# The per-layer embedding stage: ScalarE's high parts at the top of a step, the weights' high part ahead of the square

## What is computed

```python
def rmsnorm(x, g):
    xf = x.astype(jnp.float32)
    xf = xf * lax.rsqrt(jnp.mean(xf * xf, axis=-1, keepdims=True) + EPS)
    return (xf * g.astype(jnp.float32)).astype(x.dtype)

def layer(...):
    ...
    x = x + jax.nn.sigmoid(rmsnorm(x, lw['ple_norm']) @ lw['ple_w_gate']) * (p_in @ lw['ple_w_proj'])
```

## Time and profile before

| | |
|---|---|
| median of 3 runs | 3121.93 us (3119.97 to 3122.65) |
| the profiled execution, its own time | 3125.64 us |
| its span, first to last instruction | 3123.9 us |
| mean granted TensorE clock | 0.976 of 2.4 GHz |
| PE busy | 2988.7 us (96%) |
| DVE busy | 1580.6 us (51%) |
| ACT busy | 1137.1 us (36%) |
| embedding stage of layer 0, from its step loop to its last matmul | 1442 to 1566 us of the span |
| embedding stage of layer 1, the same | 2981 to 3105 us of the span |

### The profile page before, as it was taken

The page is one execution under the profiler, slowest core; times in us unless marked ns, Lnnn a source line. Parts: engine busy times, 40 slices in busy tenths (PEclk is TensorE's granted clock), DMA queues, the critical chain, the costliest instruction groups (busy, mean ns, idle before and its releaser), DMA issues. The chain is left out here.

```text
span 3123.9 us, 46695 instructions
## 1 busy us (share of the span) xinstructions
PE 2988.7 (96%) x19219; PEld 2813.3 (90%) x19219; DVE 1580.6 (51%) x2696; ACT 1137.1 (36%) x2148; POOL 143.3 (5%) x260
## 2 busy tenths in 40 slices
PE   6999989999999999998989999999999999999997
PEld 5998755899999999998989887559999999999997
DVE  6233644564554554456561346445645554454655
ACT  6223423443333223335452333334533233333343
POOL 0000300000000000000000003000000000000000
PEclk9999889999999999998999989999999999999998
DMA  3101243421111111112221021533211111111021
GB/s 128 41 28 45 94 152 105 150 73 55 41 55 41 46 50 54 41 46 82 89 71 41 14 94 56 182 92 137 75 53 41 55 41 55 41 41 54 33 95 70
DMA packets 70742, 215.40 MB, mean 69 GB/s; under 512 B 6522, under 2 KB 43386, under 8 KB 54146
## 3 DMA queue, kind: packets, MB, share of 16 engines
q1 hardware_dynamic: 70530, 212.42, 19.7%
HBM read 193.52 MB, written 18.87 MB: 68 GB/s over the span
## 5 line engine op out<-in xcount | busy, mean ns | idle before, releaser
L223 PE MATMUL psum<-h_chunk,out_weight_parts 128*128 128x352 f32 x2112 | 681.5, 323 | 0.0
L224 PE MATMUL psum<-h_chunk,out_weight_parts 128*128 128x352 f32 x2112 | 677.1, 321 | 0.0
L225 PE MATMUL psum<-h_chunk,out_weight_parts 128*128 128x352 f32 x2112 | 676.4, 320 | 0.0
L2233 DVE SCALAR_TENSOR_TENSOR conv_sum<-u_padded,vectors,conv_sum 128x1024 f32<-128x1024 f32 x176 | 226.3, 1286 | 540.2 <-ACT conv_sum L2085 537.1
L224 PEld LDWEIGHTS psum<-h_chunk,out_weight_parts 128*128 128x128 f32 x2112 | 396.8, 188 | 0.0
L223 PEld LDWEIGHTS psum<-h_chunk,out_weight_parts 128*128 128x128 f32 x2112 | 396.2, 188 | 0.0
L225 PEld LDWEIGHTS psum<-h_chunk,out_weight_parts 128*128 128x128 f32 x2112 | 395.8, 187 | 0.0
L223 PE MATMUL psum<-g_parts,out_weight_parts 128*128 128x352 f32 x960 | 309.3, 322 | 0.0
L224 PE MATMUL psum<-g_parts,out_weight_parts 128*128 128x352 f32 x960 | 309.0, 322 | 0.0
L225 PE MATMUL psum<-g_parts,out_weight_parts 128*128 128x352 f32 x960 | 308.8, 322 | 0.0
L2259 DVE TENSOR_TENSOR x<-x,psum 128x352 f32<-128x352 f32 x528 | 254.9, 519 | 94.3 <-PE psum L225 94.0
(11 more groups left out here) (356 smaller groups left out, 5511.8 us busy)
## 6 DMA issues: line engine op xcount, KB each, us to landing
out_weight_stage<-w_up_dram SPq DMA_DIRECT2D x44, 1024.0 KB, 4.8
out_weight_stage<-w_down_dram SPq DMA_DIRECT2D x22, 1024.0 KB, 4.7
mix_weight_stage<-w_in_dram SPq DMA_DIRECT2D x18, 1024.0 KB, 4.9
pages<-cache_dram SPq DMA_DIRECT2D x64, 288.0 KB, 4.6
out_weight_stage<-w_out_dram SPq DMA_DIRECT2D x16, 1024.0 KB, 6.4
out_weight_stage<-w_gate_dram SPq DMA_DIRECT2D x16, 1024.0 KB, 4.8
pages<-cache_dram SPq DMA_DIRECT2D x64, 160.0 KB, 2.7
x<-x_in_dram SPq DMA_DIRECT2D x6, 1408.0 KB, 11.1
```

Source lines behind the costliest of these rows:

```text
L223: pe.matmul(out, lhs[0], rhs[0], start=first, stop=False)
L224: pe.matmul(out, lhs[0], rhs[1], start=False, stop=False)
L225: return pe.matmul(out, lhs[1], rhs[0], start=False, stop=last)
L2233: dve.scalar_tensor_tensor(t[:, q, 0:SEQ], row[:, tap:tap + SEQ], w, t[:, q, 0:SEQ], ALU.mult, ALU.add).then_inc(ph["conv_step"], 1)
```

## The change

In ACT's step loop of `layer_embedding`, the `high` pairs and `p_high` stand at the top of a step, ahead of the wait for `gate_made` and the sigmoid, where they stood behind the sigmoid, the square and the weights' high part. And `weights_high` stands directly behind the sigmoid, ahead of `square(s - 1)`, where it stood behind it. No instruction is added or removed, and PE, DVE, POOL and SP issue what they issued, in the same order. (Lines of the loop move: the sigmoid is L2596 before and L2606 in the changed kernel.)

```diff
             for s in range(S):
-                act.wait_ge(ph["gate_made"], s + 1)
-                if s >= 2:
-                    act.wait_ge(ph["x_made"], s - 1)
-                act.activation(sg[:, s % 2, :], ps[:, s % 4, 0:CH], ACT.Sigmoid).then_inc(ph["sg_made"], 1)
-                if s:
-                    square(s - 1)
-                if s in (1, 3, 9, 11, 17, 19):
-                    weights_high({1: 3, 3: 4, 9: 5, 11: 6, 17: 7, 19: 8}[s])
                 if s in (2, 4, 5, 6):
                     k = {2: 0, 4: 2, 5: 4, 6: 6}[s]
                     high(1, (k, k + 1))
@@
                     high(2, (k, k + 1))
                 if s == 14:
                     p_high(2)
+                act.wait_ge(ph["gate_made"], s + 1)
+                if s >= 2:
+                    act.wait_ge(ph["x_made"], s - 1)
+                act.activation(sg[:, s % 2, :], ps[:, s % 4, 0:CH], ACT.Sigmoid).then_inc(ph["sg_made"], 1)
+                if s in (1, 3, 9, 11, 17, 19):
+                    weights_high({1: 3, 3: 4, 9: 5, 11: 6, 17: 7, 19: 8}[s])
+                if s:
+                    square(s - 1)
                 if s in (12, 20):
                     norm.root(act, s // KX - 1, s // KX + 1)
```

## The result

The changed kernel takes 3106.47 us (median of 5 runs, 3104.22 to 3111.33) against 3122.65 us of the kernel before (median of 5, 3119.97 to 3124.14): a ratio of 0.995, with a 95% interval of 0.9939 to 0.9961. That is 0.5% faster, 16.2 us. The profiled execution took 3111.33 us itself, with a span of 3109.5 us and a mean granted clock of 0.978; it is the slowest of its five, and I come back to that.

The account below looks back on a forecast made before the run. PE, busy for 96% of the span, was taken as the bound, with gaps waiting on DVE's low parts. Gains of 9.9 + 2.2 + 1.4 + 1.8 = 15.3 us took 3121.93 to 3106.6, range 3102.5 to 3112.0.

Parts of the forecast that it names:

- every sign named as right: No gap at step 8, about 2.2 us at step 16, no DVE idle before L2629, none at L395, stages 7 to 8 shorter.
- Step 8, layer 0: PE's gap at the first gate matmul of step 8 goes entirely: 3.47 + 1.65 us in layer 0.
- the spread: Spreads of the norm: PE's waits for the inverted roots go, 1.8 us together, bounds 0 and 1.8.
- The walk through the steps: Layer 0, DVE's work counted forward: step 6's last low pair ends near 1473.4; PE wants it at 1475.97.
- the spare time: Before step 8, the last low pair is ready 2.6 us ahead of PE's need, as cover for DVE delays.
- Step 16, layer 0: PE's gap at chunk 2's start only shrinks from 3.31 to 2.2 us, 2.2 gained over both layers.
- Ends of the stages: Both embedding stages' ends hang on the last `added` and move with PE; no gain of their own.
- the clock term: Slow clock behind step 16's gap avoided at one of two places: 1.4 us, bounds 0 to 2.8.
- The table load: ACT's root: load taken as the row's 1.28 us; with the skill's 2.66, some 14 us gained instead of 15.3.
- A (DVE stays behind): Rival: a handover eats the spare time, step 8's gap only shrinks, spreads stay; gain 5 to 11 us; chance 0.14.
- B: Rival: PE's gaps are not DVE's, for instance sequencer code fetch at a chunk's start; 3121.9 us; chance 0.05.
- C: Rival: high pairs delay ACT's sigmoid in six steps, DVE waits in `added`; 9 us slower, 3131; chance 0.03.

## Why the prediction was right

The time, 3106.47 us, is the forecast's 3106.6 and well inside the range, and every sign named as right is there: the last matmul of a stage, too, stands 7.5 us closer to its first in layer 0 and 8.3 us in layer 1. Step by step, with the stages cut at the same matmuls of both traces:

- **Step 8, layer 0.** From the start of step 0 to the spread behind step 13: 1511.09 - 1445.28 = 65.81 before, 60.00 now, 5.81 gained. The sum had 3.47 + 1.65 for the gap and 0.63 for the spread, 5.75. In layer 1 it was 65.43 before and is 59.97, 5.46 gained, where the sum had 3.14 + 1.65 + 0.64 = 5.43. The walk through the steps held too: the last low pair of step 6 ends at 1472.52 + 1.07 = 1473.59, predicted 1473.4; of the weights' low part of step 3 the walk had DVE free at 1461.3, and the next instruction starts at 1461.84, which is 0.3 us late when the 0.21 by which the stage starts later is taken off; DVE's wait for PE in the next steps hides it. PE's step 8 starts at 1476.19, so the spare time is 2.6 us, as predicted.
- **Step 16, layer 0.** From the first spread to the second: 44.78 before, 43.15 now, 1.63 gained; the sum had 1.1 + 0.49 and no clock for a place where it falls, 1.59. The remaining gap of 2.12 us was predicted as 2.2. The reason given for it, that DVE cannot run ahead in step 15, holds for the work behind `normed`, but not for the low pair itself, as the 2.02 us of idle time ahead of `normed(15)` show.
- **The rest of layer 1**, from the spread of step 13 to the final norm: 60.01 before, 57.20 now, 2.81 gained, of 1.1 and the clock term of 1.4, 2.5.
- **The exit of layer 0** was mis-sized. "Ends of the stages ... move with PE", that is nothing of their own, but from the second spread to the mixing it was 21.08 and is 20.11, 0.97 gained. In step 23 DVE used to be late: `normed` started straight behind other work. Now it waits for PE (both rows are DVE's timeline, the first of before, the second of the changed kernel):

```profile
1565.93 0.53 DVE L2644 TENSOR_TENSOR psum<-psum,inverse_row 128x352 f32<-128x352 f32 x1
```

```profile
1557.75 0.53 DVE L2644 TENSOR_TENSOR psum<-psum,inverse_row 128x352 f32<-128x352 f32 x1 [0.18 <-PE psum L225]
```

PE's last matmul starts at 1565.63 in the one and at 1558.35 in the other. DVE's tail stood 0.9 us closer to PE, and the mixing with it (idle time 11.00 to 10.08). With only the high parts moved it is 10.90, so this belongs to the weights' part.

- **The clock.** I took one of two places, and the profiled execution shows one of two. Over all traces falls are rarer: the clock fell behind 4 of 20 gaps of 2.12 us, and behind 1 of 16 without the kernel with the pair in step 7. The changed kernel's layer 0 takes 123.26 us with the fall and 121.98 and 121.76 in the two executions without, so a fall costs 1.3 to 1.5, as the earlier trace rows had it. But the sum also took a fall behind each of the four gaps of before, from one execution, and in the two kernels that keep gaps of 3.31 us it came behind two of four. By these rates, 6 of 8 and 4 of 20, the clock gives back some 4 x 0.75 x 1.6 - 2 x 0.2 x 1.4 = 4.2 us, an estimate, where the sum had 1.65 + 1.65 + 1.4 = 4.7: two errors that nearly cancel. The Trainium skill (TensorE: Matmul & The Clock Gate, Part 1) has the gate's window run free of the program; the runs agree in that one gap of 2.12 us, in one kernel, was followed by a fall in one execution and by none in the next two.
- **The table load.** The sum went by the row and was right not to add 1.4 us: in the changed kernel the root starts 1.30 us behind the start of its load, and the spread has no idle time. Timeline of ACT:

```profile
1502.01 0.50 ACT L420 ACTIVATE embedding_squares<-x 128x352 f32<-128x352 f32 x1 [1.01 <-DVE norm L429]
1502.52 1.28 ACT L384 ACT_TABLE_LOAD   x1
1503.82 0.26 ACT L384 ACTIVATE out_norm_columns<-psum,constants 128x3 f32<-128x3 f32 x1
```

Of the 2.66 us for each switch by the Trainium skill (ScalarE: Activation LUTs, What ACT_TABLE_LOAD costs) the load's own 1.28 us show here; the rest, which it puts down to a drain, does not: the load starts at 1502.52, 0.01 us behind the end of the square, and the root 0.02 us behind the end of the load.

- **The rivals.** A (DVE stays behind) fell in that either half alone clears step 8. The spare time of 2.6 us needs both, though: with the high parts alone the last pair ends at 1470.93 for a step 8 that starts at 1472.43, 1.5 us, and with the weights alone about 0.1 is left. B fell with the two kernels that move the last pair by a step, C with the late sigmoid. C's price was too high in any case: only step 4 of its six has the embedding input's 0.78 us beside the pair.

The medians differ by 16.2 us and the sum was 15.3; with the exit that it left out, 0.9, it is 16.2 too. The two stages of the profiled pair alone gained 16.7, and its spans differ by 14.4 only because the unchanged part ran 2.1 us longer. That the forecast hit to 0.1 us is luck: the gain was 0.9 too small and the kernel before, set at 3121.93, came out 0.7 higher in the runs beside the changed one, while the changed kernel's three medians alone lie 0.8 us apart.

What makes the unchanged part differ by 9.0 us between executions can be read from the traces in the main. Windows of 4 us over it show 96 to 113 us at the lower clock in the 14 executions, and 89 to 95 us in which PE is not busy. With half of the first and all of the second taken off, the rest is 2705.1 to 2707.5 us: the 9.0 have shrunk to 2.4. What stays open is why the clock falls in one execution and not in the next, behind the like gap, and why idle time elsewhere varies by some 5 us.

## What to carry to other kernels

Where an engine's gap has no releaser in the profile, look for the instruction of another engine that ends a tenth of a microsecond before it; then go back from it to what *its* input waited behind. Here that was a square, wanted by nobody for two steps, that waited for the very engine which then waited for the part behind it: put what others need in front of an instruction that has to wait. And give an operand that is due at a chunk's start a place one step before the last, since behind the last step's own product nothing hides it. Compare kernels that differ by a few microseconds by the length of the changed stage between two fixed instructions.

## What the runs showed of the hardware

Like gaps do not have like consequences for TensorE's clock: behind PE's idle 3.31 or 2.98 us the granted clock fell to 0.5 in 6 of 8 cases, behind 2.12 us in 4 of 20. And the same code, some 2850 us of it, took 2846.3 to 2855.4 us in different executions; between these two some 6.8 of the 9.0 us are the lower clock (99 and 113 us at it).
